# Decoder layer on one core: key steps of the sample's attention made in pairs from step 32 on

## What is computed

```python
def diff_attention_rows(q, q_pos, k, v, lam):
    s = jnp.einsum('bqhce,bkhce->bhcqk', q.astype(jnp.float32), k.astype(jnp.float32)) * (e ** -0.5)
    ...
    a = jax.nn.softmax(jnp.where(mask, s, -jnp.inf), axis=-1)
    attn = a[:, :, 0] - lam * a[:, :, 1]
    return jnp.einsum('bhqk,bkhe->bqhe', attn, v.astype(jnp.float32))
...
    past_k = pool_k[page_table].reshape(b, PAST_LEN, B_HEADS, 2, HEAD_DIM)
    past_v = pool_v[page_table].reshape(b, PAST_LEN, B_HEADS, B_VDIM)
```

## Time and profile before

| | us |
|---|---|
| median of 3 runs (1440.95 to 1441.73) | 1441.09 |
| the profiled execution | 1440.92 |
| its span | 1439.2 |
| PE busy, of the span | 1376.7 (96%) |
| DVE busy | 937.3 (65%) |
| ACT busy | 556.5 (39%) |
| GpSimd busy | 245.0 (17%) |

### The profile page before, as it was taken

How to read it: one execution, slowest core, us unless ns; L and a number is a source line. 1 busy time by engine, 2 the same in 40 slices (tenths; PEclk the granted TensorE clock), 3 DMA queues, 4 the chain that set the end, 5 groups by cost and what they waited for, 6 DMA issues and landing times.

```text
span 1439.2 us, 27725 instructions
## 1 busy us (share of the span) xinstructions
PE 1376.7 (96%) x10683; PEld 1158.2 (80%) x10683; DVE 937.3 (65%) x1685; ACT 556.5 (39%) x1104; POOL 245.0 (17%) x268
## 2 busy tenths in 40 slices
PE   4999999999999999998999999999989999999997
PEld 4788998899998878884666666667889988899986
DVE  2222483589965656545556666658899974899848
ACT  4322342044542422124454444444554431345520
POOL 1000220155500000001110111000054500455200
PEclk8999999999999999999999999999999999999999
DMA  9998263133333143356899999993123324333431
GB/s 313 373 376 295 74 189 119 37 110 89 95 119 110 26 137 106 119 188 235 288 348 372 345 377 336 378 366 115 52 74 89 111 81 134 94 89 94 127 117 66
DMA packets 183021, 257.75 MB, mean 179 GB/s; under 512 B 11419, under 2 KB 103329, under 8 KB 182890
## 3 DMA queue, kind: packets, MB, share of 16 engines
q1 hardware_dynamic: 182890, 255.97, 52.8%
HBM read 248.05 MB, written 7.88 MB: 178 GB/s over the span
## 4 chain that ended last, share of the span: by engine, by line
PE 78%; DVE 11%; DMA 3%; issue 3%; ACT 3%; SPq 1%; POOL 0%; DVEq 0%; ACTq 0%
PE ps L1242 20%; PE ps L596 19%; PE ps L1887 8%; PE ps L2290 6%; PE ps L340 6%; PE ps L2356 3%; PE ps L2302 3%; PE ps L600 3%; DVE ring_lo L1234 3%; PE ps L2383 2%; PE ps L1630 2%; DMA wada<-in_w_ada_dram 1%; PE ps L1874 1%; PE ps L2400 1%; PE ps L324 1%
## 5 line engine op out<-in xcount | busy, mean ns | idle before, releaser
L1234 DVE TENSOR_TENSOR ring_lo<-ring_raw,ring_hi 128x512 fp32r<-128x512 f32 x293 | 263.9, 934 | 67.0 <-ACT ring_hi L1222 64.8
L1222 ACT ACTIVATE ring_hi<-ring_raw 128x512 fp32r<-128x512 f32 x326 | 187.4, 620 | 162.4 <-DMA ring_raw<-in_ffn_w_out_dram 93.8
L596 PE MATMUL ps<-ring_hi,f 128*128 128x512 f32 x704 | 217.2, 390 | 0.0
L1242 PE MATMUL ps<-hhi,ring_hi 128*128 128x288 f32 x588 | 176.1, 300 | 6.4 <-DVE tmp L1449 3.0
L1242 PE MATMUL ps<-hlo,ring_hi 128*128 128x288 f32 x588 | 174.3, 296 | 0.0
L596 PEld LDWEIGHTS ps<-ring_hi,f 128*128 128x128 f32 x704 | 131.9, 188 | 27.0
L2290 PEld LDWEIGHTS ps<-ident,k_ring 128*128 128x128 f32 x832 | 89.1, 141 | 61.1 <-issue 36.5
L596 PE MATMUL ps<-ring_lo,f 128*128 128x512 f32 x352 | 137.2, 390 | 0.0
L1242 PE MATMUL ps<-hhi,ring_lo 128*128 128x288 f32 x456 | 135.2, 296 | 0.0
L2290 PE MATMUL ps<-ident,k_ring 128*128 128x128 f32 x832 | 121.6, 282 | 7.7 <-ACT KC L2507 4.1
L1242 PE MATMUL ps<-sumhi,ring_hi 128*128 128x288 f32 x396 | 118.7, 300 | 6.1 <-DVE tmp L1449 4.3
(11 more groups left out here) (295 smaller groups left out, 2870.5 us busy)
## 6 DMA issues: line engine op xcount, KB each, us to landing
wada<-in_w_ada_dram SPq DMA_DIRECT2D x18, 2048.0 KB, 14.1
ring_raw<-in_ffn_w_in_dram SPq DMA_DIRECT2D x140, 256.0 KB, 3.0
k_ring<-in_cache_diff_k_dram SPq DMA_DIRECT2D x128, 256.0 KB, 4.9
ring_raw<-in_ffn_w_out_dram SPq DMA_DIRECT2D x88, 256.0 KB, 3.3
v_rest<-in_cache_diff_v_dram SPq DMA_DIRECT2D x72, 256.0 KB, 4.6
k_ring<-in_cache_win_k_dram SPq DMA_DIRECT2D x16, 768.0 KB, 7.1
w<-in_w_qkv_dram SPq DMA_DIRECT2D x21, 512.0 KB, 3.8
w<-in_ffn_w_in_dram SPq DMA_DIRECT2D x18, 512.0 KB, 8.4
```

The lines of the kernel that those rows point to most:

```text
L596: m = nc.tensor.matmul(ps[:, bank, :], x, w, start=(first and n == 0), stop=(last and n == 2), skip_group_check=True)
L1222: eng.activation(hi_of(g, i)[:], raw_of(g, i)[:], ACT.Copy).then_inc(sem("g_hi"), 1)
L1234: eng.tensor_tensor(lo_of(g, i)[:], raw_of(g, i)[:], hi_of(g, i)[:].bitcast(F32), ALU.subtract).then_inc(sem("g_lo"), 1)
L1242: m = nc.tensor.matmul(ps[:, bank, 0:TH], w, x, start=(first and n == 0), stop=(last and n == 2), skip_group_check=True)
```

## The change

Up to step 31 the loop stays, with four alterations. The prompt scores of the first two query blocks (128 and 256 keys) run on all 128 rows, head after head, against a query tile `QP` whose other half is zero. The new keys' products with the first chunk of a sequence also run on all 128 rows, rows 64 to 127 of `PTd[:, NPAGE]` and `V[:, :, PT_]` being zero (memsets on GpSimd). In steps 13, 15, 21, 23, 29 and 31 the prompt transposes stand ahead of the third key block instead of behind the fourth (`TURN_EARLY`). And on DVE the last `top` of a unit and the unit's maximum (`unit_top`) move from the end of step 7 of the unit behind the first copy of the next step.

From step 32 on two steps n and n + 1 are made as one: eight key blocks with prompt transposes, prompt scores and weights between them, then the values of two steps, then the scores of two steps. The odd step's keys are copied to a second place, `KD`, the prompt keys of mixer A in `KT`, which are read for the last time in step 30. Values run one step later for even steps (n - 10 and n - 9 in one pair), so value step 54 moves behind the loop. Loads of values are put into SP's order by the pair in which the slots come free. The output transposes, prompt values and the mean of a head move to other steps of the unit.

```diff
+        KD = [KT[:, f, 0:NPR] for f in range(4)]
...
+        DOUBLE = STEPS // 2
...
+        def values_in(n):
+
+            return [v for v in (n - LAG - 1, n - LAG) if v >= DOUBLE - LAG]
...
+        def value_done(v):
+
+            return v + LAG + 1 if v < DOUBLE - LAG else 2 * ((v + LAG + 1) // 2) + 2
+
+        def keys_copy(n):
+            return KD if n >= DOUBLE and n % 2 else KC
...
+        TURN_EARLY = tuple(n for n in range(UNIT, STEPS // 2) if n % UNIT in (5, 7))
...
                 for v in range(AHEAD, STEPS - LAG):
-                    if freed_steps(value_step, v) == done - LAG:
+                    if value_done(freed_steps(value_step, v) - 1) == done:
                         load_values(v)
...
-                            pe.matmul(ps[32 * f:32 * f + 32, out_bank(w), 0:P], PTd[0:NSM, NPAGE, 32 * f:32 * f + 32],
-                                      V[0:NSM, m, PT_, f * P:(f + 1) * P], start=False, stop=False,
+                            pe.matmul(ps[32 * f:32 * f + 32, out_bank(w), 0:P], PTd[:, NPAGE, 32 * f:32 * f + 32],
+                                      V[:, m, PT_, f * P:(f + 1) * P], start=False, stop=False,
...
+                whole = q < 2 and n > 0
...
+                    if whole:
+                        pe.matmul(ps[:, 5 + h, 0:w], QP[:, h, q % 2, :], KT[:, b, 0:w], start=True, stop=True).then_inc(sem("p_score"), 1)
...
-            for n in range(STEPS):
+            for n in range(DOUBLE):
...
-                if n in SCORES_LATE:
+                if n in SCORES_LATE or n in TURN_EARLY:
                     prompt_turn(n - 1, v)
...
+            for n in range(DOUBLE, STEPS, 2):
+                b, i = divmod(n, UNIT)
+                turned_now = [v for v in values_in(n) if v % UNIT < 4]
+                turn_keys(n, 0)
+                turn_keys(n, 1)
+                prompt_turn(n - 1, n - LAG - 2)
+                for w in out_in(n - 2):
+                    turn_out(w)
+                turn_keys(n, 2)
+                turn_keys(n, 3)
+                prompt_scores(n)
+                for v in turned_now[0:1]:
+                    turn_weights(v)
+                turn_keys(n + 1, 0)
+                turn_keys(n + 1, 1)
+                for v in turned_now[1:2]:
+                    if v % UNIT == 1:
+                        turn_new(v // UNIT)
+                    turn_weights(v)
+                turn_keys(n + 1, 2)
+                turn_keys(n + 1, 3)
+                for v in values_in(n):
+                    values(v)
+                if i == 0:
+                    scores_new(n)
+                scores(n)
+                scores(n + 1)
...
-            prompt_turn(STEPS - 1, STEPS - LAG)
+            prompt_turn(STEPS - 1, STEPS - LAG - 2)
+            values(STEPS - LAG - 1)
             values(STEPS - LAG)
...
-                    eng.wait_ge(sem("d_sc"), n)
-                eng.activation(KC[f][:, 0:w], ps[:, 0, 0:w], ACT.Copy).then_inc(sem("d_kca"), 1)
+                    eng.wait_ge(sem("d_sc"), n - (n > DOUBLE))
+                if f == 0 and n == DOUBLE + 1:
+                    eng.wait_ge(sem("p_score"), DOUBLE)
+                eng.activation(keys_copy(n)[f][:, 0:w], ps[:, 0, 0:w], ACT.Copy).then_inc(sem("d_kca"), 1)
...
+            for n in range(DOUBLE, STEPS, 2):
+                b, i = divmod(n, UNIT)
+                evacuate(n, 1)
+                for w in out_in(n - 2):
+                    keep_out(w)
+                if i == 0:
+                    unit_top(b - 1)
+                evacuate(n, 3)
+                prompt_top(n)
+                evacuate(n + 1, 1)
+                prompt_top(n + 1)
+                if i == 2:
+                    invert_sum(b - 1)
+                    prompt_out(b - 1)
+                evacuate(n + 1, 3)
+                prompt_norm(n)
+                prompt_norm(n + 1)
+                for w in out_in(n):
+                    weigh_out(w)
+                if i == 0:
+                    new_scores(b)
+                    new_top(b)
+                if i < UNIT - 2:
+                    top(n + 1)
```

More of the change, by code:

```diff
@@ L2139, in out_of, with out_in @@
             return (n - 13) // 4 if n % 4 == 1 and n >= 13 else None
+        def values_in(n):
+            return [v for v in (n - LAG - 1, n - LAG) if v >= DOUBLE - LAG]
+        def out_in(n):
+            return [v // 4 for v in values_in(n) if v % 4 == 3]
+        def value_done(v):
+            return v + LAG + 1 if v < DOUBLE - LAG else 2 * ((v + LAG + 1) // 2) + 2
+        def keys_copy(n):
+            return KD if n >= DOUBLE and n % 2 else KC
         def out_bank(w):
@@ L2461, in attend_tensor @@
                     prompt_scores(n)
-                elif n > 0 and is_turn(mixer_of((n - 1) // UNIT), (n - 1) % UNIT):
+                elif n > 0 and n not in TURN_EARLY and is_turn(mixer_of((n - 1) // UNIT), (n - 1) % UNIT):
                     prompt_turn(n - 1, v)
```

115 lines of the change are left out of this document (80 added, 35 removed).

## The result

The changed kernel takes **1446.04 us** (median) against 1442.92 for the kernel before: ratio 1.0029, 95% interval 1.0018 to 1.0041. It is slower by 3 us in the medians (about 4 by the ratio); the forecast was 11.5 us faster, with 1437 as the upper end of its range. The profiled execution has a span of 1442.6 us against 1439.2.

The account below looks back on a forecast made before the run. The prediction took TensorE (PE) to set the pace, with transfers close behind. Its terms, 3.0 + 11.7 - 2.0 - 1.2 = 11.5 us gained, gave 1429.4 us against the profiled execution, 1429.6 against the median; range 1424 to 1437.

Parts of the forecast that it names:

- What bounds the kernel: Steps 32 to 63: PE sets the pace, busy 146.95 of 153.3 us; it waits for no load yet.
- little room behind it: Steps 32 to 63: DMA share already 0.94 to 1.01, rate 330 to 382 GB/s, close behind PE.
- Rows at full depth: New keys' products on 128 rows: about 0.25 us gained a sequence, 1.5 before step 32 and 2.0 after.
- First half: Steps 0 to 31: 3.0 us gained from fuller rows, prompt scores and moved transposes, less 0.3 for the unit's maximum.
- the early transposes: Steps 13, 15, 21, 23, 29, 31: prompt transposes before the third block gain 1.7 us, after 0.25 lost twice.
- Pairs on PE: Steps 32 to 63: PE's line 11.7 us shorter, units 4 to 7 at 31.5, 39.0, 32.3 and 38.8.
- the bank's return: Pairs from step 32: the wait for a bank's copy-out, 8 x 0.42 us uncovered, half covered elsewhere; no gain taken.
- Loads: Steps 32 to 63: 2.0 us of new PE waits, narrowest at value steps 29, 31, 45, 47; ends 0 and 8.
- The end of the stage: Behind the last scores: output weights arrive 18.3 us later instead of 17.1, 1.2 us lost, behind the load for value step 56.
- transfers are the bound: Rival: 382 GB/s is all there is, so units 5 and 7 cannot shrink; 1432.5 us, chance 0.20.
- SP's queue stands still: Rival: SP's waits for values delay keys at pair starts; slower from 14.7 us of waits, 1444.5 at 1.1 each; chance 0.07.
- The pair only moves the waits to DVE and ACT: Rival: late copies make PE wait 0.48 us at the third block in all 16 pairs, 7.7 us; 1437.3, chance 0.07.

Follow-up runs that it names:

- light_before: The kernel before with the loads of value steps 5 to 57 cut to half their bytes; 1439.60 us, ratio 0.9980.
- no_early_turn: The changed kernel with the prompt transposes of steps 13, 15, 21, 23, 29 and 31 back behind the fourth key block; 1447.88 us (one run).
- fixed_light: The changed kernel with fixed pages in units 5 and 7 (no page-number reads by SP there) and half the bytes of most value loads; 1436.67 us (one run).
- fixed_after: The changed kernel with fixed pages in units 5 and 7, so SP reads no page numbers there; 1443.58 us, ratio 1.0010.
- values_first: The changed kernel with a pair's two value loads put ahead of the key load that its second step frees; 1441.59 us, ratio 0.9997.
- both_orders: The changed kernel with the load orders of values_first and tail_order together; 1437.69 us, ratio 0.9966.
- tail_order: The changed kernel with the loads for value steps 59 and 60 put ahead of that for 56; 1439.16 us, ratio 0.9974.
- split_tail: The changed kernel with a pair's first values before its second step's third block, load 59 ahead of 56 and 60 ahead of 57; 1437.39 us, ratio 0.9965.
- early_tail: The changed kernel with page numbers for the next pair's keys read before the values' wait, and loads 59 and 60 ahead of 56; 1437.30 us, ratio 0.9966.
- single_steps: The changed kernel without the pairs, every step from 32 on made singly as before; 1438.85 us, ratio 0.9976.

## Why the prediction was wrong, step by step

*What bounds the kernel* was right: light_before shows that PE alone set the pace and that transfers were just hidden. The warning that there was "little room behind it" was the whole case, and I priced it at 2.0 us.

*Rows at full depth*: right. Each sequence gains 0.27 (steps 9, 13, 17, 21, 25 and 29, at 21 beside the gain of the transposes; predicted 0.25).

*First half*, 3.0 predicted, 1.5 measured (1.8 with light loads). The term that failed is the early transposes, 1.7: no_early_turn gives 0.72. At steps 13, 15, 29 and 31 nothing is left of what was to be saved. I expected scores that wait for the copy at 15 and 31 and charged 0.25; it is all of it, and at 13 and 29 too. Steps 8 and 16, with the unit's maximum behind the copy, are 0.45 longer instead of 0.3, and the prompt scores of 256 columns cost 0.09 each, as priced.

*Pairs on PE*, 11.7 predicted, 6.9 measured with the loads out of the way: the worked pair is right to the hundredth and, piece by piece, to 0.05 (46 and 47: 9.37 predicted, 9.37 in the changed kernel). Units 5 and 7 are 0.6 and, cut alike, 0.8 us longer than priced (39.6 and 39.0). Units 4 and 6 were priced 3.4 us too short (33.3 and 33.9 for 31.5 and 32.3). "I take no gain there" for the bank's return was too kind: in the window units a block is only two or three tiles. PE in fixed_light, unit 4:

```profile
808.22 0.27 PE L2380 MATMUL ps<-ident,S 128*64 128x128 f32 x1
809.15 0.63 PE L2372 MATMUL ps<-ident,S 128*128 128x128 f32 x4 [0.66 <-ACT PTd L2616]
...
825.30 0.44 PE L2327 MATMUL ps<-ident,k_ring 128*128 128x128 f32 x2 [0.26 <-ACT KT L2584]
825.89 0.44 PE L2327 MATMUL ps<-ident,k_ring 128*128 128x128 f32 x2 [0.15 <-DVE KT L2693]
```

The second weights of a pair wait 0.66 for the copy of the first's, and two transposes (0.22) cover a third of a bank's return. Pair 34, predicted at 7.3, takes 8.09, pair 50 8.03. These waits (0.66 in the pairs 34 and 50, 0.26 and 0.15 in 38 and 54) come to 2.1 of the 3.4 us; the rest is spread over the pairs and was not traced further.

*Loads*, 2.0 predicted, 7.9 measured: at the end of the range 0 to 8. The cause (slots free by twos, a load for values behind two for keys) and two of the four places were right. The term that failed is the 0.9 us for which the key load ahead was to hold SP. The slot for value step 29 is free when the values of the pair before are done. Here are the scores that follow those values, and the landing of the load (issues, KB each, median us), first in the changed kernel, then in fixed_after:

```profile
820.74 0.83 PE L2330 MATMUL ps<-KC,QB 128*32 128x384 f32 x8
v_first<-in_cache_diff_v_dram SPq DMA_DIRECT2D x4, 256.0 KB, 5.0
```

```profile
822.37 0.83 PE L2333 MATMUL ps<-KC,QB 128*32 128x384 f32 x8
v_first<-in_cache_diff_v_dram SPq DMA_DIRECT2D x4, 256.0 KB, 6.0
```

The load goes out 2.4 us behind the free slot (823.15 - 820.74), at value step 45 3.5 (900.40 - 896.94); the landing is as priced. Together the tiles come 9.4 and 10.8 us behind the free slot, predicted 7.0 to 9.0 (for value step 47), and PE needs them after 7.2 and 7.5, priced at 7.7. But the hold is not the only cause: in fixed_after it is 0.2 us at value step 29, and the tiles still come 9.4 us behind the free slot (0.4 and 9.6 at step 45). A reading that fits, and that no run tests by itself, is the time before the burst: I priced issue and landing from the earlier trace rows, where transfers flow, while in the changed kernel they run dry for some 4 us (the missing shares, 0.55 and 0.24, of 5 us each), and 16 tiles go out ahead of this load. Taking the reads away gives 1.6, half of the values' bytes 4.6, both 7.9, the order 3.7: these overlap, and no one of them is the share of one cause. Once the order is better, units 5 and 7 stand at 41.0 to 41.7 us in values_first and both_orders with DMA shares of 1.00 to 1.04: the rival "transfers are the bound" fits just these units in these runs. Its rate did not hold: tail_order has 394 GB/s over unit 7. The ceiling of about 358 GB/s that the prediction quoted is, in the Trainium skill's words on the roofline (Perfetto Trace Analysis, section Roofline under Engine Utilization), the share of a core when both cores of a pair use the memory; it says that a core alone can pull more, and the trace agrees with that, not with the ceiling.

*The end of the stage*, 1.2 predicted, 5.3 measured. The mechanism was named (the load for value step 56 waits for value step 52); the term was mis-sized. Its own sum is off as well: 7.3 MB at 400 GB/s, 2 us of landing and 2.4 us of head start make 17.9 us, not 18.3, so 0.8. I filled the transfers from 2.4 us before the last scores on, as if they came there with a full queue; SP stood for 6.7 us ahead of that point, with the loads 59 and 60 behind the waiting one, though tail_order has both out before 948.5. For the fall of the clock I had no term: 0.75 us of the 5.3, and 1.4 more behind the mark for seven products at 1.2 GHz (0.20 each).

*The sum*: 1.5 + 6.9 - 7.9 - 5.3 - 0.6 = -5.4 us, the traces' difference, against 3.0 + 11.7 - 2.0 - 1.2.

*The rivals.* "SP's queue stands still" came nearest in time (1444.5), but with 14.7 us of waits to be found, where PE waited 5.9 us for loads in steps 32 to 63; its break-even leaves out the 1.2 us lost at the end, and with them it is 13.5. Its place was wrong: keys at the start of each pair. The stands of SP that the late loads follow lie in the middle of units 4 and 6 and at the end, each for values. "The pair only moves the waits to DVE and ACT" is out: PE's waits for their copies in these steps are 3.5 us, before 4.8.

What stays open: how the 3.4 us of the order and the 4.5 us that are left in both_orders (153.8, 150.3, 145.8) divide between queue depth and rate, since no kernel here has the pairs with transfers that never run dry; that would take more slots.

Best of all were split_tail, early_tail and both_orders, 1437.3 to 1437.7 (0.9965 to 0.9966), not to be told apart from each other. single_steps, without pairs, is 1.2 to 1.6 us behind, and its interval overlaps theirs; whether pairs in a better order beat single steps is not shown.

## What to carry to other kernels

Where PE sets the pace and the DMA share is already 0.97, work taken off PE may not shorten the stage, since the transfers are close behind: take half of the bytes away in a trial kernel, in the version before and after, and the two bounds stand side by side. Doing two steps' work at one point also frees their buffers at one point; look, in the queue that refills them, for what has a free slot and stands behind a load that has not, and put it ahead. A wait on PE can cost more than itself, since the products behind it may run at 1.2 GHz for a while: 3.25 and 4.56 us did here.

## What the runs showed of the hardware

SP's reading of four page numbers takes 1.53 us, almost as much as the four issues behind it (1.9); yet taking it away moved the tiles of value step 29 by 0.02 us and those of step 45 by 1.1.

How long PE waits does not settle alone whether its clock falls. At value step 29 waits of 2.2 us left it at 1.00 (the changed kernel, fixed_after); at step 45 a wait of 2.11 did not. PE in fixed_after there, and a window behind it:

```profile
907.58 1.11 PE L2388 MATMUL ps<-v_first,PTd 128*32 128x128 f32 x32 [2.11 <-DMA v_first<-in_cache_diff_v_dram]
```

```profile
910.00:912.00 2.00, 2.00 (x12) 1.67 (x9) 0.00 (x0) 0.52 (x1) 0.00 (x0) 0.52 1.08 390
```

Where PE waits for no load, a trace is exact to some 0.02 us: the kernel before with all bytes and with light loads agree so well in every unit, and gains of 0.27 a step can be read from one trace each.
